# The last feature tile's position parts: 384 and 128 instead of 256 and 256, and the last 128 output rows in two pieces

## The reference

```python
def swiglu(h, w_gate, w_up, w_down):
    g = jnp.einsum('bsd,df->bsf', h, w_gate)
    u = jnp.einsum('bsd,df->bsf', h, w_up)
    return jnp.einsum('bsf,fd->bsd', jax.nn.silu(g) * u, w_down)
...
        x = x + swiglu(h, ffn_w_gate[i], ffn_w_up[i], ffn_w_down[i])
    return rmsnorm(x, norm_final)
```

## Time and profile before

| What | Value |
|---|---|
| Median of 3 runs | 2913.97 us (2910.84 to 2914.2) |
| Profiled execution, its own time | 2914.81 us |
| Its span in the trace | 2913.0 us |
| PE busy | 2881.1 us (99% of the span) |
| DVE, ACT, POOL busy | 1113.1, 1075.2, 1172.3 us |
| Part 0 of tile 7 begins on PE | 2886.55 us |
| Part 1 of tile 7 begins on PE | 2894.47 us |
| Last matmul of tile 7 begins | 2904.90 us |

### The profile page before, as it was taken

The page is one execution under the profiler, slowest core; times in us unless marked ns, Lnnn a source line. Parts: engine busy times, 40 slices in busy tenths (PEclk is TensorE's granted clock), DMA queues, the critical chain, the costliest instruction groups (busy, mean ns, idle before and its releaser), DMA issues.

```text
span 2913.0 us, 34009 instructions
## 1 busy us (share of the span) xinstructions
PE 2881.1 (99%) x14291; PEld 2370.1 (81%) x14291; DVE 1113.1 (38%) x1783; ACT 1075.2 (37%) x1607; POOL 1172.3 (40%) x499
## 2 busy tenths in 40 slices
PE   8999999999999999999999999999999999999999
PEld 5787888888888877888898888888888877788888
DVE  6433582466664534322242211532221256522211
ACT  4335333343323424432343332342222366432222
POOL 2332354344444532444444444444444423344442
PEclk9999999999999999999999999999999999999999
DMA  8422363346564422333333333333333322233332
GB/s 256 119 87 64 108 188 108 88 156 198 188 195 141 113 58 62 84 94 95 101 88 100 95 96 95 97 95 96 95 98 95 104 66 66 73 100 95 95 96 77
DMA packets 511244, 314.92 MB, mean 108 GB/s; under 512 B 16210, under 2 KB 482804, under 8 KB 510836
## 3 DMA queue, kind: packets, MB, share of 16 engines
q1 hardware_dynamic: 511092, 312.75, 36.1%
HBM read 310.61 MB, written 2.10 MB: 107 GB/s over the span
## 4 chain that ended last, share of the span: by engine, by line
PE 96%; DVE 2%; SPq 1%; ACT 1%; DMA 0%; issue 0%; DVEq 0%; ACTq 0%
PE b L439 23%; PE b L441 23%; PE b L440 23%; PE o L439 6%; PE o L440 6%; PE o L441 6%; PE s L762 1%; PE o L877 1%; DVE aP L2743 1%; PE b L1056 1%; PE b L1057 1%; PE b L1058 1%; PE s L857 1%; PE s L1204 0%; PE b L490 0%; PE b L491 0%
## 5 line engine op out<-in xcount | busy, mean ns | idle before, releaser
L2886 POOL TENSOR_TENSOR lo<-raw,hi 128x1024 fp32r<-128x1024 f32 (+1 forms) x489 | 1170.0, 2400 | 1706.0 <-ACT hi L1318 1705.7
L439 PE MATMUL b<-HH,hi 128*128 128x512 f32 x1912 | 760.5, 398 | 0.8 <-ACT GT L1702 0.8
L441 PE MATMUL b<-HH,lo 128*128 128x512 f32 x1912 | 745.5, 390 | 0.0
L440 PE MATMUL b<-HL,hi 128*128 128x512 f32 x1912 | 745.3, 390 | 0.0
L1318 ACT ACTIVATE hi<-raw 128x1024 fp32r<-128x1024 f32 (+1 forms) x492 | 508.5, 1038 | 373.4 <-DMA raw<-in_w_down_dram 98.9
L439 PEld LDWEIGHTS b<-HH,hi 128*128 128x128 f32 x1912 | 359.3, 188 | 84.1 <-issue 7.7
L440 PEld LDWEIGHTS b<-HL,hi 128*128 128x128 f32 x1912 | 359.5, 188 | 76.2 <-issue 2.4
L441 PEld LDWEIGHTS b<-HH,lo 128*128 128x128 f32 x1912 | 359.3, 188 | 75.8
L439 PE MATMUL b<-FH,hi 128*128 128x512 f32 (+1 forms) x594 | 222.3, 374 | 0.0
L441 PE MATMUL b<-FH,lo 128*128 128x512 f32 (+1 forms) x594 | 221.7, 373 | 0.0
L440 PE MATMUL b<-FL,hi 128*128 128x512 f32 (+1 forms) x594 | 221.7, 373 | 0.0
(11 more groups left out here) (508 smaller groups left out, 3923.6 us busy)
## 6 DMA issues: line engine op xcount, KB each, us to landing
raw<-in_w_up_dram SPq DMA_DIRECT2D x88, 512.0 KB, 3.9
raw<-in_w_in_dram SPq DMA_DIRECT2D x80, 512.0 KB, 4.1
raw<-in_w_ada_dram SPq DMA_DIRECT2D x80, 512.0 KB, 4.8
raw<-in_w_mg_dram SPq DMA_DIRECT2D x48, 512.0 KB, 3.8
raw<-in_ffn_w_gate_dram SPq DMA_DIRECT2D x44, 512.0 KB, 3.9
raw<-in_ffn_w_up_dram SPq DMA_DIRECT2D x44, 512.0 KB, 3.9
raw<-in_w_down_dram SPq DMA_DIRECT2D x32, 512.0 KB, 3.7
raw<-in_ffn_w_down_dram SPq DMA_DIRECT2D x32, 512.0 KB, 3.7
```

Of the source, the lines that this page charges most:

```text
L439: e.matmul(out, wh, xh, start=start and k == 0, stop=False)
L440: e.matmul(out, wh, xl, start=False, stop=False)
L441: mm = e.matmul(out, wl, xh, start=False, stop=stop and k == last)
L2886: e.tensor_tensor(t["lo"][:, s, 0:w], K.raw[:, s, 0:w], t["hi"][:, s, 0:w].bitcast(F32), ALU.subtract).then_inc(*m.lo.up(n))
```

## The change

Tile 7 of the last projection is cut at position 384 instead of 256: part 0 has blocks 0 to 2, part 1 only block 3. Everything that goes with a part follows: the sums, the root and the reciprocal of part 0 are for 3 blocks, of part 1 for 1. Blocks 0, 1 and 2 are turned, emptied and stored during part 1, block 3 after it. The pieces of finish come one point later than before: the sums after 24 matmuls of part 1 (before: 12), the turns after 48 (before: 36). DVE and ACT each empty their half of block 3 in two pieces of 256 columns, and SP stores block 3 with two DMAs, the first of which takes the first piece of both halves: 2 x 128 runs of 256 f32 (1 KB) each. The other blocks are stored as before, in runs of 4 KB.

The core of the diff (the edits in x_update, add_late, square and weigh only hand cols_of its new argument, and the scalar and vector out_proj change `steps` as the tensor one does):

```diff
@@ -128,8 +128,16 @@
     return "w" if d < WHOLE[nid] else hf
 
 
-def cols_of(part):
-    return slice(0, S) if part == "w" else slice(256 * part, 256 * part + 256)
+def edge_of(nid):
+    return 384 if nid == 8 else 256
+
+
+def cols_of(nid, part):
+    return slice(0, S) if part == "w" else slice(edge_of(nid), S) if part else slice(0, edge_of(nid))
+
+
+def blocks_of(nid, hf):
+    return range(edge_of(nid) // 128, 4) if hf else range(edge_of(nid) // 128)
 
 
 def halves_of(hf):
@@ -572,8 +580,8 @@
         st = self.bank[b]
         q.wait_ge(m.vnorm.at("ss", nid, 6, part_of(nid, 6, hf)), m.anorm.at("sq", nid, 7, part_of(nid, 7, hf)),
                   self.free[b])
-        for r in range(2):
-            c = slice(256 * hf + 128 * r, 256 * hf + 128 * r + 128)
+        for r, block in enumerate(blocks_of(nid, hf)):
+            c = slice(128 * block, 128 * block + 128)
             e.matmul(st[:, r:r + 1], t["SS"][:, c], t["ones"][:, 0:1], start=True, stop=False)
             mm = e.matmul(st[:, r:r + 1], t["SQ"][:, 1, c], t["ones"][:, 0:1], start=False, stop=True)
         mm.then_inc(*m.stat.up(("sum", nid, hf)))
@@ -1069,9 +1077,9 @@
             self.free[b] = m.vnorm.at("x", nid, d, "w")
         held = {d: list(entries(d)) for d in range(halves, KD)}
         self.half_left = kt == 8
-        steps = 2 if self.half_left else 3
+        steps = 2 if self.half_left else 4 if nid == 8 else 3
         for hf in range(2):
-            c = halves_of(hf)
+            c = cols_of(nid, hf)
             for d in held:
                 b = self.take_bank(("out", nid, d, hf))
                 for n, k0, kn, hi, lo in held[d]:
@@ -1273,24 +1281,22 @@
             b = TURN_BANKS[r][u]
             q.wait_ge(free[b])
             for k in range(4 * u, 4 * u + 4):
-                q.wait_ge(m.vnorm.at("y", 1) if r >= 2 and k == 7 else m.anorm.at("y", k, part_of(8, k, r // 2)))
+                q.wait_ge(m.vnorm.at("y", 1) if r == 3 and k == 7 else m.anorm.at("y", k, part_of(8, k, 0)))
                 mm = e.transpose(bank[b][:, (k % 4) * 128:(k % 4) * 128 + 128], t["X"][:, k, r * 128:r * 128 + 128],
                                  t["ident"][:, :])
             mm.then_inc(*m.stat.up(("turned", i)))
             free[b] = m.anorm.at("row_out", i) if u else m.vnorm.at("row_out", i)
 
+        yield None
         self.sums(8, 0)
         yield None
         yield None
-        turn(0, 0)
-        turn(0, 1)
-        turn(1, 0)
-        turn(1, 1)
-        yield None
-        turn(2, 0)
+        for r in range(3):
+            turn(r, 0)
+            turn(r, 1)
+        yield None
         turn(3, 0)
         self.sums(8, 1)
-        turn(2, 1)
         turn(3, 1)
 
 
@@ -1950,22 +1956,24 @@
 
         def store(r):
             i = 2 * r + 1
-            q.wait_ge(m.stat.at("turned", i), m.vnorm.at("r", 8, r // 2))
-            e.activation(t["OT"][:, r, 512:1024], bank[TURN_BANKS[r][1]][:, :], ACT.Copy,
-                         scale=t["RS"][:, r:r + 1]).then_inc(*m.anorm.up(("row_out", i)))
+            q.wait_ge(m.stat.at("turned", i), m.vnorm.at("r", 8, r // 3))
+            for c0, n, key in ((0, 256, "begun"), (256, 256, "row_out")) if r == 3 else ((0, 512, "row_out"),):
+                e.activation(t["OT"][:, r, 512 + c0:512 + c0 + n], bank[TURN_BANKS[r][1]][:, c0:c0 + n], ACT.Copy,
+                             scale=t["RS"][:, r:r + 1]).then_inc(*m.anorm.up((key, i)))
 
         def root(hf):
-            self.rstd(bank[("t1", "s1")[hf]], 2, D, m.stat.at("sum", 8, hf), t["RS"][:, 2 * hf:2 * hf + 2],
-                      m.anorm.up(("sd", 8, hf)))
-
+            blocks = blocks_of(8, hf)
+            self.rstd(bank[("t1", "s1")[hf]], len(blocks), D, m.stat.at("sum", 8, hf),
+                      t["RS"][:, blocks[0]:blocks[-1] + 1], m.anorm.up(("sd", 8, hf)))
+
+        yield None
         root(0)
         yield None
         yield None
-        store(0)
-        store(1)
+        for r in range(3):
+            store(r)
         yield None
         root(1)
-        store(2)
         store(3)
 
 
@@ -2034,7 +2042,7 @@
     def x_update(self, nid, d, part, gate):
 
         e, q, m, t = self.e, self.q, self.m, self.t
-        c = cols_of(part)
+        c = cols_of(nid, part)
         X = t["X"]
         out = self.out_of(("out", nid, d, part))
         q.wait_ge(m.dense.at("out", nid, d, part))
@@ -2846,26 +2854,29 @@
 
         def store(r):
             i = 2 * r
-            q.wait_ge(m.stat.at("turned", i), m.vnorm.at("r", 8, r // 2))
-            e.tensor_scalar(t["OT"][:, r, 0:512], bank[TURN_BANKS[r][0]][:, :], t["RS"][:, r:r + 1], None,
-                            ALU.mult).then_inc(*m.vnorm.up(("row_out", i)))
+            q.wait_ge(m.stat.at("turned", i), m.vnorm.at("r", 8, r // 3))
+            for c0, n, key in ((0, 256, "begun"), (256, 256, "row_out")) if r == 3 else ((0, 512, "row_out"),):
+                e.tensor_scalar(t["OT"][:, r, c0:c0 + n], bank[TURN_BANKS[r][0]][:, c0:c0 + n], t["RS"][:, r:r + 1], None,
+                                ALU.mult).then_inc(*m.vnorm.up((key, i)))
 
         def root(hf):
-            RS = t["RS"][:, 2 * hf:2 * hf + 2]
+            blocks = blocks_of(8, hf)
+            RS = t["RS"][:, blocks[0]:blocks[-1] + 1]
             q.wait_ge(m.anorm.at("sd", 8, hf))
             e.reciprocal(RS, RS).then_inc(*m.vnorm.up(("r", 8, hf)))
 
+        yield None
         root(0)
         yield None
         yield None
-        store(0)
-        store(1)
+        for r in range(3):
+            store(r)
         yield None
         q.wait_ge(m.anorm.at("sq", 8, 7, 1))
-        e.tensor_scalar(t["X"][:, 7, 256:S], t["X"][:, 7, 256:S], t["PAR"][:, 551:552], None, ALU.mult).then_inc(
+        c = cols_of(8, 1)
+        e.tensor_scalar(t["X"][:, 7, c], t["X"][:, 7, c], t["PAR"][:, 551:552], None, ALU.mult).then_inc(
             *m.vnorm.up(("y", 1)))
         root(1)
-        store(2)
         store(3)
 
 
@@ -2953,9 +2964,14 @@
         if n == K.tags["attn"] + 6:
             attn_tables()
         chunk(n)
-    for r in range(4):
+    for r in range(3):
         q.wait_ge(m.vnorm.at("row_out", 2 * r), m.anorm.at("row_out", 2 * r + 1))
         e.dma_start(K.out[0, r * 128:r * 128 + 128, :], t["OT"][:, r, :]).then_inc(*m.stored[r].up(0))
+    quarters = lambda x: x.rearrange("p (u i c) -> p u i c", u=2, i=2)
+    for i, key in enumerate(("begun", "row_out")):
+        q.wait_ge(m.vnorm.at(key, 6), m.anorm.at(key, 7))
+        e.dma_start(quarters(K.out[0, 384:512, :])[:, :, i, :], quarters(t["OT"][:, 3, :])[:, :, i, :]).then_inc(
+            *m.stored[3 + i].up(0))
     q.wait_ge(*[s.at(0) for s in m.stored])
 
 
```

More of the change, by code:

```diff
@@ L217, in __init__ @@
         self.ba = Mark(sem("gla_bias_loaded"), 16)
-        self.stored = [Mark(sem(f"rows_stored{i}"), 16) for i in range(4)]
+        self.stored = [Mark(sem(f"rows_stored{i}"), 16) for i in range(5)]
     def all(self):
@@ L1408, in weigh @@
     def weigh(self, nid, d, part):
-        t, c = self.t, cols_of(part)
+        t, c = self.t, cols_of(nid, part)
         if nid == 8 and (d, part) != (7, 1):
@@ L2058, in add_late @@
             dd, pp, before = self.late
-            c = cols_of(pp)
+            c = cols_of(nid, pp)
             q.wait_ge(m.anorm.at("sq", nid, dd, pp), before)
```

## The result

| | before | after |
|---|---|---|
| Median, 22 runs each | 2912.70 us (2910.66 to 2914.75) | 2918.97 us (2914.05 to 2922.49) |
| Ratio | | 1.0019, 95% interval 1.0014 to 1.0025 |
| Profiled execution, its span | 2913.0 | 2916.3 |
| Part 0 of tile 7, first product to part 1's | 7.92 | 11.46 |
| Part 1, first product to last | 10.43 | 14.52 |

The ratio is 5.5 us and the medians lie 6.27 us apart: a small slowdown, but its interval leaves 1 out. The forecast was +2.27 us and 2916.2, in a range of 2912.0 to 2919.5. Tile 7 begins 2.71 us earlier in the profiled execution after (2883.84) than before (2886.55), and the change touches nothing ahead of it; so I compare from tile 7 on, where the change costs +6.01 us, close to the medians.

A forecast was written before the change was run, and what follows sets the result against it. PE, busy 99% of the span, then a serial 8.10 us tail bound the kernel. PE +4.41, tail up to the factor -0.73, behind it -1.41: +2.27 us, median about 2916.2, range 2912.0 to 2919.5.

The forecast's parts named there:

- Part 0, 384 wide: Tile 7's part 0: 66 products at 0.1735 us instead of 0.120, costing +3.53 us.
- Part 1's pace: Part 1's 128-wide products: weight loads set the pace, 0.111 us each instead of 0.120, -0.59 us in all.
- (a): Part 1: narrow products go by columns, 0.067 us each, loads do not bind; total -0.6 us, 2913.3; chance 0.10.
- (b): Part 1: 81 ns a product, loads partly overlapping one another; total +0.3 us, 2914.2; chance 0.08.
- the prediction's own sign: Prediction counts as wrong if part 1's pace is under 0.10 or over 0.13, or the tail over 7 us.
- Rival (c): Part 1: narrow products fall to plain f32 pace, 0.226 us each; total +9.9 us, 2923.8; chance 0.09.
- The sum of part 1: Part 1, first product to last, with added sums, turns and wait: 10.43 + 0.88 us.
- The wait for bank t: Part 1's turns: PE wants reused bank t 0.07 us too early; taken as +0.15 us, ends 0 and 0.9.
- Tail up to the factor: Last product to the end of the reciprocal: 2.80 us before, shortened by 0.73 to 2.07.
- Tail behind the factor: Emptying and storing block 3 after the reciprocal: 3.89 us instead of 5.30, so -1.41, ends -1.6 and -0.6.
- The 0.79 from issue to data: Block 3's final store: 0.79 us between issuing the DMA and its data starting to move.
- rival (d): Block 3's store: its pieces end no sooner than one 512 KB store; total +3.1 us, 2917.0; chance 0.08.

The follow-up runs named there:

- the kernel with nothing between: Changed kernel, but sums, turns and stores of blocks 0 to 2 all follow part 1's last product: 2915.45 us, ratio 1.0008.
- the sums moved: Changed kernel, with the three blocks' sums put directly ahead of the turns, behind 48 narrow products instead of 24: 2916.79 us, ratio 1.0014.
- kernels with 208 columns: Changed kernel, part 1's products run over 208 positions: 2915.84 us; the same with block 3 stored by two DMAs in 2 KB runs: 2916.08 us.
- those with 256 columns: Changed kernel, but part 1's products run over 256 positions although only the last 128 are used: 2916.79 us, ratio 1.0012.
- one store: Changed kernel, but block 3 is emptied whole by each engine and stored with one DMA in 4 KB runs: 2917.10 us, ratio 1.0018.
- the sums three times over: Kernel before (256 and 256), with part 0's sums made three times over within part 1: 2915.81 us, ratio 1.0008.

## Why the prediction was right, and where it was not

The range held the time, and "a little slower, by less than 0.2%" is what came, but the size was +5.5 us (+0.19%) and not +2.27. That the range held is in part luck. The forecast stood on a median of three runs, 2913.97, and the 22 runs put the kernel before at 2912.70; from 2913.97, the measured 6.27 us would have ended at 2920.2, outside. And the range was not made wide for what came: neither the clock nor the slower start of the store is among its terms. By its steps:

- **Part 0, 384 wide**: right. 11.46 us for 66 products, 0.1736 each, against 0.1735; it costs 3.54 us over before.
- **Part 1's pace**: right as long as the clock held, 0.111. Rivals (a) and (b), 0.067 and 0.081, did not come. The Trainium skill (TensorE: Matmul & The Clock Gate, "Back-to-back issue gap") gives 81 ns for a width of 128; this case's traces do not agree, with 111. By the prediction's own sign (wrong over 0.13) the pace was wrong for the 18 products at 0.213. Rival (c), the plain pace, looked as if it had come: the 0.213 at 2900.01 is near its 0.226 (the prediction's rows give 0.22; where the 0.226 comes from is not said). It is the clock, since the same products ran at 0.111 before and behind, and all 66 do in the kernel with nothing between.
- **The sum of part 1**: 11.31, measured 14.52 in the changed kernel and 11.31 in the profiled execution with the sums moved, where the clock held. The 3.2 us are the term that the prediction did not have. The wait for bank t, taken at 0.15, came to about 0.05 in the changed kernel: the turn into t began 0.49 behind the one into o (2906.99 to 2907.48) instead of 0.44, helped by the slow clock ahead of it. With the clock up, in the kernels with 208 and 256 columns and the one with the sums moved, it is 0.57, a wait of 0.13, as forecast. For a transpose the prediction takes 0.109 and works out 1.66 us for 16, which is 0.104; the starts of the turns, 0.44 apart, give the 0.109, and the difference is 0.04 us in all.
- **Tail up to the factor**: right, 2.10 against 2.07.
- **Tail behind the factor**: 3.89 forecast, 4.38 measured (2911.92 to 2916.3). The data's 1.50 was right (1.53). The 0.79 from issue to data was the mis-sized term, taken from stores of 128 runs of 4 KB; with 256 runs of 1 KB it is 1.31. Against the kernel before, 0.92 came back behind the factor, between the 1.41 of the forecast and the 0.6 of rival (d).
- **In all**: 2.27, plus 3.2 for the clock, plus 0.5 for the store, is 6.0, what the trace shows from tile 7 on.

The step that failed is the silent one: the prediction took a clock of 1.00 over all of tile 7, as it was in the kernel before, for granted; the runs showed 0.50 for 6.8 us of part 1, which cost 3.2 us. The change replaced products that stream columns for 0.107 of every 0.120 us (256 columns by the step that the prediction read) by ones that stream 0.053 of 0.111. The prediction had worked out just this and drew only the conclusion on the pace. It is not the whole reason, though: 66 such products with nothing between them did not lower the clock. The same page of the Trainium skill ("HAM oscillation — how this bites in real kernels") ties such falls to gaps in which PE is idle; here PE had none, so that rule would not have warned.

How settled this is: that the fall costs what is missing is shown (with 256 or 208 columns the clock held and 2.6 to 3.1 us of part 1 came back). What goes before a fall was seen in one profiled execution of each kernel, and that is thin: in the stretches near 2424 and 2496 the same code met a fall in one execution and none in another. The times help for two kernels only, those with 256 columns and with nothing between, whose 11 times lie close together. The changed kernel's spread (8.4 us over 22 runs, 4.1 before) and its two profiled relatives (6.8 us at half clock, 3.4 with one store) say that the fall does not come to the same length in every execution. What decides within one kernel, and whether the sums and the narrow products are needed together or only make a fall likelier, stays open.

## What to carry to other kernels

Before narrowing a matmul that brings its own weights, find where its load sets the pace: here at about 0.111 us, which by the slope of the wider ones (0.053 for 128 columns) should be met near 230 columns, and everything narrower only adds to its partner's cost. Then ask what the stretch does to the clock, one-column sums and narrow products together; padding the narrow product up to the load's pace cost 0.07 us (11.38 against 11.31) and left the clock up in both profiled executions of kernels with 208 columns, though one of 22 times looks like a fall. Before you compare two profiles, look where each was at half clock: here two such stretches that the change does not touch were worth 3.2 us, more than the whole forecast. A last store that is cut into more runs may start later than the whole one.

## What the runs showed of the hardware that was not expected

- PE's granted clock went to half while PE was busy without a gap: in the changed kernel for 6.8 us, in the one with the sums three times over for 3.4 us.
- It also went to half in code that both kernels share, in some executions and not in others; each such stretch of 3.4 us cost 1.6 us.
- 66 products of 128 columns in a row (7.20 us) did not lower it.
- SP took 0.64 us for a DMA of 256 runs of 1 KB and 0.33 for one of 128 runs of 4 KB; from issue to data it was 1.31 and 0.80 us.
